# One-column norm sums and a scaled identity that spreads the root, in a kernel of four stacked layers

## The reference

```python
def rmsnorm(x, g):
    y = x * lax.rsqrt(jnp.mean(x * x, axis=-1, keepdims=True) + EPS)
    return y * g

# layers 0 and 1: sh, sc, gate vectors come from silu(c) @ ada_w + ada_b
h = modulate(rmsnorm(x, norm1_g), sh1, sc1)          # h * (1 + sc) + sh
x = x + g1 * (gated Fourier branch + gated retention branch)(h) @ w_out
h = modulate(rmsnorm(x, norm2_g), sh2, sc2)
x = x + g2 * conv_ffn(h)                             # after layer 1: x = rmsnorm(x, final_g)

# layers 2 and 3: the same form of norms, for x and (mostly) for the context
p, u, vs, q, k, v, gates = split(modulate(rms_norm(x, norm1_g), sh1, sc1) @ w_in)
x = x + g1 * (pool mix + spatial gating + neighbourhood attention, gated)(...) @ w_o
x = x + g2 * square(relu(modulate(rms_norm(x, norm2_g), sh2, sc2) @ w1)) @ w2
return rms_norm(x, final_g)
```

## Time and profile before

| what | value |
|---|---|
| median of 3 runs | 2119.51 us (2118.06 to 2119.61) |
| span of the profiled execution | 2116.1 us |
| what lies around the span | the page gives the span alone, no total time of this execution |
| PE busy | 2080.5 us, 98% |
| DVE busy | 1496.3 us, 71% |
| ACT busy | 987.6 us, 47% |
| POOL busy | 392.7 us, 19% |
| mean granted TensorE clock | 0.992 |
| HBM read | 393.09 MB, 186 GB/s over the span |

### The profile page before, as it was taken

How to read it: one execution, slowest core, us unless ns; L and a number is a source line. 1 busy time by engine, 2 the same in 40 slices (tenths; PEclk the granted TensorE clock), 3 DMA queues, 4 the chain that set the end, 5 groups by cost and what they waited for, 6 DMA issues and landing times.

```text
span 2116.1 us, 36942 instructions
## 1 busy us (share of the span) xinstructions
PE 2080.5 (98%) x14236; PEld 1916.5 (91%) x14236; DVE 1496.3 (71%) x2161; ACT 987.6 (47%) x1501; POOL 392.7 (19%) x288
## 2 busy tenths in 40 slices
PE   8999999999999999999999999999999989999998
PEld 7999999999999999999877888888888988999998
DVE  5876888877777899978988524897533466866554
ACT  4444456544445566553245523432232245755453
POOL 0330203210511213224101102130010031121020
PEclk8999999999999999999999999999999999999999
DMA  7876767686675666664544322456632244564552
GB/s 285 293 253 199 253 221 250 239 288 214 213 239 197 212 199 216 197 233 132 184 165 146 108 85 87 137 182 229 197 101 91 81 158 160 203 214 160 183 186 100
DMA packets 109594, 396.36 MB, mean 187 GB/s; under 512 B 12408, under 2 KB 13056, under 8 KB 109056
## 3 DMA queue, kind: packets, MB, share of 16 engines
q1 hardware_dynamic: 108160, 389.99, 54.7%
q0 software_dynamic: 1280, 4.20, 0.6%
HBM read 393.09 MB, written 1.05 MB: 186 GB/s over the span
## 4 chain that ended last, share of the span: by engine, by line
PE 84%; DVE 11%; DMA 2%; ACT 2%; issue 1%; POOL 0%; DVEq 0%; SPq 0%; POOLq 0%; ACTq 0%
PE bank L486 21%; PE bank L488 21%; PE bank L487 21%; DVE w_lo L1435 5%; PE bank L587 2%; PE bank L585 2%; PE bank L586 2%; DMA stage<-in_stream 1%; PE bank L661 1%; PE bank L658 1%; DVE stage L1456 1%; PE bank L606 1%; DVE rstd L1453 1%; PE bank L509 1%; PE bank L877 1%
## 5 line engine op out<-in xcount | busy, mean ns | idle before, releaser
L1435 DVE TENSOR_TENSOR w_lo<-stage,w_hi 128x1024 fp32r<-128x1024 f32 x536 | 705.0, 1330 | 457.2 <-ACT w_hi L1004 456.9
L1004 ACT ACTIVATE w_hi<-stage 128x1024 fp32r<-128x1024 f32 x536 | 565.7, 1059 | 849.0 <-PE bank L488 599.9
L486 PE MATMUL bank<-h_hi,w_hi 128*128 128x256 f32 (+1 forms) x2560 | 788.5, 308 | 6.8 <-DVE w_lo L1435 4.1
L487 PE MATMUL bank<-h_lo,w_hi 128*128 128x256 f32 (+1 forms) x2560 | 782.9, 306 | 0.0
L488 PE MATMUL bank<-h_hi,w_lo 128*128 128x256 f32 (+1 forms) x2560 | 782.9, 306 | 0.0
L486 PEld LDWEIGHTS bank<-h_hi,w_hi 128*128 128x128 f32 x2560 | 489.8, 191 | 36.5 <-DVE w_lo L1435 7.4
L487 PEld LDWEIGHTS bank<-h_lo,w_hi 128*128 128x128 f32 x2560 | 489.8, 191 | 21.6 <-issue 0.5
L488 PEld LDWEIGHTS bank<-h_hi,w_lo 128*128 128x128 f32 x2560 | 489.7, 191 | 21.5
L1456 DVE SCALAR_TENSOR_TENSOR stage<-stage,cvec 128x1024 f32<-128x1024 f32 x188 | 253.8, 1351 | 4.2 <-DMA stage<-in_stream 1.7
L486 PE MATMUL bank<-f_hi,w_hi 128*128 128x256 f32 (+1 forms) x448 | 147.3, 329 | 0.0
L488 PE MATMUL bank<-f_hi,w_lo 128*128 128x256 f32 (+1 forms) x448 | 146.7, 327 | 0.0
(11 more groups left out here) (254 smaller groups left out, 3272.2 us busy)
## 6 DMA issues: line engine op xcount, KB each, us to landing
stage<-in_stream SPq DMA_DIRECT2D x728, 512.0 KB, 4.3
bias<-in_bias POOLq DMA_DIRECT2D x16, 256.0 KB, 3.2
X<-in_x SPq DMA_DIRECT2D x2, 1024.0 KB, 7.0
cvec<-in_cvec SPq DMA_DIRECT2D x3, 512.0 KB, 4.1
decay<-in_decay SPq DMA_DIRECT2D x1, 1024.0 KB, 5.4
out<-X SPq DMA_DIRECT2D x4, 256.0 KB, 2.1
rope<-in_rope SPq DMA_DIRECT2D x2, 256.0 KB, 4.9
wsgu<-in_wsgu SPq DMA_DIRECT2D x2, 256.0 KB
```

The source lines that it names most:

```text
L486: mm(out, w_hi[:, slot, w], xh[:, c, 0:T], start=first, stop=False)
L487: mm(out, w_hi[:, slot, w], xl[:, c, 0:T], start=False, stop=False)
L1004: A(w_hi[:, m % NR, :], stage[:, n % NS, :], ACT.Copy).then_inc(hi_ready, 1)
L1435: do(V.tensor_tensor(w_lo[:, m % NR, :], stage[:, n % NS, :], w_hi[:, m % NR, :].bitcast(F32), ALU.subtract), unit_done, done_value(n))
```

## The change

A norm's sum is taken as one column for each half of its 256 tokens, and not as a row spread over all partitions.

- norm_sums: for each source chunk two products take the place of one, with 128 tokens of the squares as the stationary side and one column of mean_D as the moving one. The result is 128 tokens (on partitions) by 2 columns. The number of source chunks, GpSimd's adds and the waits on them stay.
- root works on 2 columns, and so does the reciprocal. VectorE then writes diag: the identity times the reciprocal column, for each half of the tokens (two tensor_scalar products of 128x128).
- spread_root, new on TensorE: ones (128x128) as the stationary side by diag (256 columns) puts the root of every token in all partitions of a second bank. So each norm has two groups where it had one.
- scaled and final_norm read the root from that bank (root_of); after the eighth chunk VectorE copies one element (root_used) to release it. For the first norm keep_root copies it to rstd, and the chunks read rstd.
- The identity is loaded in SyncE's prologue, behind X and ahead of the weight stream, no longer with the tables of layer 2 (`loaded2` counts 48 where it was 64).
- Where there is padding, 16 products become 4, the spread, and 5.
- The hooks: in dn1 the sums stay before unit 4 and the spread stands before unit 5; in pu of layer 2 nf's sums move one output chunk ahead, from (0, 0, 2) to (0, 0, 1), with the spread at (0, 0, 3); in pu of layer 3 the sums of c1 move from before unit 3 to before unit 2, with the spread before unit 3. The other hooks stay and have the spread two output chunks behind.

In the diff below, the places where only `loaded2` changes are left out.

```diff
-        s = [("n1", 0, 1)]
+        s = [("n1", 0, 2)]
...
-        s += [("wo0", 4, 4), ("wo1", 4, 4), ("n2", 0, 1)]
+        s += [("wo0", 4, 4), ("wo1", 4, 4), ("n2", 0, 2)]
...
-            s += [("nf", 0, 1)]
+            s += [("nf", 0, 2)]
         return s
-    s = [("c1", 0, 1), ("n1", 0, 1)] if layer == 2 else [("n1", 0, 1), ("c1", 0, 1)]
+    s = [("c1", 0, 2), ("n1", 0, 2)] if layer == 2 else [("n1", 0, 2), ("c1", 0, 2)]
...
+        std = sb("std", [P, 2, 2])
+        rcol = sb("rcol", [P, 2, 2])
+        junk = sb("junk", [1, 16])
...
-        std = sb("std", [P, T2], F32, tmp + 16 * KB)
+        diag = sb("diag", [P, 2, 2, P], F32, tmp + 16 * KB)
...
             sp.dma_start(X[:, 0, :, :], t["x"][:, 0, :, :]).then_inc(s["x_loaded"], 16)
+            sp.dma_start(ident[:, :], t["ident"]).then_inc(s["ident_in"], 16)
             for n in range(PRO):
...
-            for dst, name in ((rope2, "rope2"), (rinv, "rinv"), (rotm, "rotm"), (ident, "ident")):
+            for dst, name in ((rope2, "rope2"), (rinv, "rinv"), (rotm, "rotm")):
                 sp.dma_start(dst.ap(), t[name]).then_inc(s["loaded2"], 16)
...
                 added = ADDS[layer, name] + 1 if ADDS[layer, name] else 0
                 open_group(g)
+
+                def add(src, first, last):
+                    for tk in range(2):
+                        at = tok.start + tk * P
+                        ins = mm(bank_of(g)[:, tk:tk + 1], src[:, at:at + P], mean_D[:, 0:1], start=first and tk == 0,
+                                 stop=last, skip_group_check=True)
+                    return ins
                 if added:
                     pe.wait_ge(s["sq_added"], ADDS_BEFORE[layer, name] + ADDS[layer, name])
-                    ins = mm(bank_of(g)[:, 0:S], mean_D[:, :], ssum[:, tok], start=True, stop=added == DC)
+                    ins = add(ssum, True, added == DC)
                     if added == DC:
                         close_group(ins, g)
                 for c in range(added, DC):
                     pe.wait_ge(s["sq_ready"], SQ_BEFORE[layer, name] + c + 1)
-                    ins = mm(bank_of(g)[:, 0:S], mean_D[:, :], sq[:, c % 4, tok], start=not added and c == 0, stop=c == DC - 1)
+                    ins = add(sq[:, c % 4, :], not added and c == 0, c == DC - 1)
                     if c == DC - 1:
                         close_group(ins, g)
                     elif not added:
                         ins.then_inc(s["sq_used"], 1)
+
+            def spread_root(layer, name):
+
+                g = grp(layer, name, 1)
+                out = open_group(g)
+                pe.wait_ge(s["diag_ready"], NORMS.index((layer, name)) + 1)
+                at = diag[:, half_of(name), :, :]
+                close_group(mm(out[:, 0:S].rearrange("p (k t) -> p k t", k=2), ones[:, :], at, start=True, stop=True), g)
 
             def fill_gap(layer, name, n):
...
             norm_sums(0, "n1")
             for n in range(PRO - 1):
                 first_modulation(n).then_inc(s["pro_used"], 1)
+                if n == 0:
+                    spread_root(0, "n1")
...
                     norm_sums(L, "n1")
-                    fill_gap(L, "in", 16)
+                    fill_gap(L, "in", 4)
+                    spread_root(L, "n1")
+                    fill_gap(L, "in", 5)
                 input_products(L, hh, hl)
...
                 norm_sums(L, "n2")
-                fill_gap(L, "up0", 16)
+                fill_gap(L, "up0", 4)
+                spread_root(L, "n2")
+                fill_gap(L, "up0", 5)
                 feature_block(L, "up0", hh, hl, S, h_ready(L, "n2"), after_norm=(L, "n2"))
...
                 feature_block(L, "dn1", u_hi, u_lo, S, nothing,
-                              before={4: lambda: norm_sums(2, "c1")} if L == 1 else None)
+                              before={4: lambda: norm_sums(2, "c1"), 5: lambda: spread_root(2, "c1")} if L == 1 else None)
...
                     half_passes(L, "pu", h_hi, h_lo, [(ctx_part, (2, "c1")), (x_part, (2, "n1"))],
-                                hooks={(0, 0, 2): lambda: norm_sums(1, "nf"), (0, 3, 0): lambda: norm_sums(2, "n1")}, fresh=(1,))
+                                hooks={(0, 0, 1): lambda: norm_sums(1, "nf"), (0, 0, 3): lambda: spread_root(1, "nf"),
+                                       (0, 3, 0): lambda: norm_sums(2, "n1"), (0, 3, 2): lambda: spread_root(2, "n1")}, fresh=(1,))
                 else:
                     feature_block(L, "pu", h_hi, h_lo, T, h_ready(L, "n1"), after_norm=(L, "n1"),
-                                  before={3: lambda: norm_sums(3, "c1")})
+                                  before={2: lambda: norm_sums(3, "c1"), 3: lambda: spread_root(3, "c1")})
...
-                    split_units(L, "wo1", h_hi, h_lo, 0, hooks={(1, 1, 0): lambda: norm_sums(2, "n2")})
+                    split_units(L, "wo1", h_hi, h_lo, 0, hooks={(1, 1, 0): lambda: norm_sums(2, "n2"), (1, 1, 2): lambda: spread_root(2, "n2")})
...
                     norm_sums(L, "n2")
-                    fill_gap(L, "f0", 16)
+                    fill_gap(L, "f0", 4)
+                    spread_root(L, "n2")
+                    fill_gap(L, "f0", 5)
...
                             half_passes(L, "f0", h_hi, h_lo, [(x_part, (2, "n2")), (ctx_part, (2, "c2"))],
-                                        hooks={(0, 2, 0): lambda: norm_sums(2, "c2")})
+                                        hooks={(0, 2, 0): lambda: norm_sums(2, "c2"), (0, 2, 2): lambda: spread_root(2, "c2")})
...
                     base = 32 * (L - 2) + 16 * half
                     feature_block(L, f"d{half}0", f_hi, f_lo, T, count("ff_ready", base))
                     if L == 2 and half:
-                        split_units(L, "d11", f_hi, f_lo, 4, hooks={(1, 5, 0): lambda: norm_sums(3, "n1")})
+                        split_units(L, "d11", f_hi, f_lo, 4, hooks={(1, 5, 0): lambda: norm_sums(3, "n1"), (1, 5, 2): lambda: spread_root(3, "n1")})
                     else:
                         feature_block(L, f"d{half}1", f_hi, f_lo, T, nothing)
                 if L == 3:
                     norm_sums(3, "nf")
+                    spread_root(3, "nf")
...
-                A(std[:, tokens_of(name)], bank_of(g)[:, 0:S], ACT.Sqrt, bias=eps[:, :]).then_inc(taken[g % 8], 1)
+                A(std[:, half_of(name), :], bank_of(g)[:, 0:2], ACT.Sqrt, bias=eps[:, :]).then_inc(taken[g % 8], 1)
...
             def invert(layer, name):
 
-                tok = tokens_of(name)
+                v = half_of(name)
                 wait_taken(dve, grp(layer, name))
                 settle()
-                do(V.reciprocal(rstd[:, tok], std[:, tok]))
+                do(V.reciprocal(rcol[:, v, :], std[:, v, :]))
+                if (layer, name) == NORMS[0]:
+                    dve.wait_ge(s["ident_in"], 16)
+                settle()
+                do(V.tensor_scalar(diag[:, v, 0, :], ident[:, :], rcol[:, v, 0:1], None, ALU.mult))
+                do(V.tensor_scalar(diag[:, v, 1, :], ident[:, :], rcol[:, v, 1:2], None, ALU.mult),
+                   s["diag_ready"], NORMS.index((layer, name)) + 1)
+
+            def root_of(layer, name):
+
+                return rstd[:, 0:S] if (layer, name) == NORMS[0] else bank_of(grp(layer, name, 1))[:, 0:S]
+
+            def keep_root():
+
+                g = grp(0, "n1", 1)
+                wait_filled(dve, g)
+                take(V.tensor_copy(rstd[:, 0:S], bank_of(g)[:, 0:S]), g)
+
+            def root_used(layer, name):
+
+                n = NORMS.index((layer, name))
+                take(V.tensor_copy(junk[0:1, n:n + 1], root_of(layer, name)[0:1, 0:1]), grp(layer, name, 1))
 
             def scaled(layer, name, c):
 
                 base, v, tok = HREADY[layer, name], half_of(name), tokens_of(name)
                 if c >= 4:
                     dve.wait_ge(s["h_ready"], base + c - 3)
-                do(V.scalar_tensor_tensor(tt[:, c % 4, tok], X[:, v, c, :], MUL[:, layer % 2, v, int(name[1]) - 1, c:c + 1],
-                                          rstd[:, tok], ALU.mult, ALU.mult), s["t_ready"], base + c + 1)
+                if c == 0 and (layer, name) != NORMS[0]:
+                    wait_filled(dve, grp(layer, name, 1))
+                ins = V.scalar_tensor_tensor(tt[:, c % 4, tok], X[:, v, c, :], MUL[:, layer % 2, v, int(name[1]) - 1, c:c + 1],
+                                             root_of(layer, name), ALU.mult, ALU.mult)
+                do(ins, s["t_ready"], base + c + 1)
+                if c == DC - 1 and (layer, name) != NORMS[0]:
+                    root_used(layer, name)
 
             def rest(layer, name, c):
...
                 invert(layer, "nf")
                 settle()
                 last_norm = layer == 3
+                wait_filled(dve, grp(layer, "nf", 1))
                 for c in range(DC):
-                    do(V.scalar_tensor_tensor(X[:, 0, c, :], X[:, 0, c, :], col("final2" if last_norm else "final1", c),
```

(7 more changed lines are left out.)

14 lines of the change are left out of this document (7 added, 7 removed).

## The result

Median of four runs 2133.53 us (2127.71 to 2136.39), against 2119.0 of the kernel before: ratio 1.0071 (95% interval 1.0059 to 1.0083), so 0.7% slower. The profiled execution has a span of 2131.4, 15.3 more than before.

A forecast was written before the change was run, and what follows sets the result against it. The prediction took TensorE, 84% of the last-ending chain, to bound the kernel. Terms 3.9 - 2.8 - 0.7 + 1.0 + 3.9 + 0.5 + 2.8 = +8.6 on 2119.51 gave 2128.1 us; own range 2124 to 2132, 8-in-10 range 2117 to 2136.

The forecast's parts named there:

- The sums cost the same: Norm sums on TensorE: four one-column records, 0.42 us, replace two wide ones, 0.43; put at 0.
- The rival that a load hides behind its neighbour: One-column products: hidden loads would bring the 240 records closer, down to 2108.7 us at 0.025 spacing; faster, chance 0.08.
- The chain: Each norm's root to first scaled chunk: 2.29 us becomes 1.60, a gain of 0.7 (0.4 to 0.9).
- the term of -2.8: Four padded norms (n2 of layers 0, 1, 3; n1 of layer 1): each 0.7 us shorter, -2.8 together.
- The end: Last norm, nf of layer 3, which ends the kernel: the same shorter chain, -0.7 us.
- Prologue: Kernel start: spread and root copy 0.8 us, earlier fall of the clock 3.1; +3.9 together.
- The clock's term: Prologue: narrow products start 3.5 us sooner, so half clock comes sooner; 3.1 us, bounds 0 and 3.5.
- c1 of layer 2: Norm beside dn1: the spread before unit 5 delays the first scaled chunk and the weight split behind it; +1.0 us.
- pu of layer 2: Fourth group waits for the bank of nf's root until eight chunks end, TensorE idling 3.6 us; +3.9, the largest term.
- f0 of layer 2: Bank wait delays the first unit by 2 us, swallowed by a later 2.39 wait; the spread stays, +0.5.
- pu of layer 3: Bank wait swallowed by existing idling, but c1's earlier sums leave one unit behind it; +2.8 us, no extra clock cost.
- The rival: More falls of the clock at padded norms or in layer 2's pu, two of five places: 2134 us, chance 0.26.

The follow-up runs named there:

- the second run: The changed kernel with std, rcol and junk placed behind the last tile, so every other tile lies where the kernel before has it: 2143.45 us.
- the third run: The changed kernel with 128 columns of mean_D instead of one in each product of a norm's sum: 2120.36 us.
- the fifth: The changed kernel with 128-column sums, layer 1's nf root copied to release its bank early, and c1's sums before unit 3 of layer 3's pu: 2112.85 us.
- the first run: The kernel before with only 128 unused bytes per partition added behind rstd, moving the tiles behind as the change does: 2110.9 us.
- the eleventh: The kernel before with the same 128 unused bytes behind rstd, measured once more: 2111.42 us.
- the fourth run: The changed kernel with layer 1's nf root copied to release its bank early, and c1's sums back before unit 3 of layer 3's pu: 2122.08 us.

## Why the prediction was right or wrong

The time lay in the range and slower was forecast, and that it lay there is luck: the norms cost 22 us where 8.6 were forecast, and tiles that moved gave 7 back. Without the 7 the time is above 2136, the end of the range, as in the second run (2143.45). Even with them it is above 2132, the end of the likeliest case's own range. Which places would cost, and by which waits, was forecast rightly; what the clock does behind narrow products was not. By its steps:

**The sums cost the same.** Right: a padded norm's ten products take 2.29 us where its five took 2.32. The rival that a load hides behind its neighbour fell: the row of 16 records above (957.76 in the timeline of pu) has 1.93 us from the first start to the last end, 112 ns from one to the next. The prologue's records of the earlier trace rows are also 112 ns apart, and 213 at half clock; the forecast's 0.106 and 0.207 divide a window by a count that takes in the records cut by its edges. The start-to-start floor of 25 ns of the Trainium skill (TensorE: Matmul & The Clock Gate, "Wait — 56ns, not 53.3ns?") is far below what these rows have.

**The chain.** Direction right, size wrong: 0.7 forecast, 0.39 measured at full clock (root to first scaled chunk 1.90 for the 2.29 of the earlier trace rows). The timeline of layer 1's padded norm n1:

```profile
495.72 0.26 ACT L1079 ACTIVATE std<-bank,eps 128x2 f32<-128x2 f32 x1 [0.24 <-PE bank L607]
496.01 0.17 DVE L1537 RECIPROCAL rcol<-std 128x2 f32<-128x2 f32 x1 [0.80 <-ACT std L1079]
...
496.85 0.67 PE L629 MATMUL bank<-diag,ones 128*128 128x256 f32 x2 [0.16 <-DVE diag L1542]
...
497.62 1.26 DVE L1567 SCALAR_TENSOR_TENSOR tt<-X,MUL,bank 128x256 f32<-128x256 f32 x3 [0.93 <-PE bank L629]
```

The root takes 0.26 and not 0.20, diag starts the spread 0.14 after it ends, and from the spread to the first chunk it is 0.77, not 0.64. Two of the four padded norms gained 0.43 and 0.51; the other two, with the clock down, lost 0.65 and 0.45, so the term of -2.8 came out at +0.2. Where the clock stays up, in the third run, the four gain 0.32 to 0.41 each, half of the 0.7. The end gave 0.47 for 0.7. The chunks that read PSUM take 475 ns where those from SBUF took 480, so that they cost nothing more was right. The dearer PSUM source of the Trainium skill (VectorE: DVE Perf Modes, "The TRN2 errata") does not show in these rows.

**Prologue.** +3.9 forecast, +6.4 measured. The step that failed is the clock's: it falls near 10 and not near 12 (0.75 in the window from 8 to 12 is two of its four us at the lower level; before, still had 1.00 to 15.3). The clock's term was 3.1 with a bound of 3.5; from the third run to the changed kernel the stretch grows by 6.1. An estimate from the rows: 5.4 us of narrow work, some 48 records at 112 ns, now ran at 213, which is 4.9 more. What the spread and the copy (0.8 forecast) cost besides cannot be read from the table. The stretch is +0.25 in the third run and +1.85 in the fifth, with the same prologue, and +0.38 and +0.14 in the first and the eleventh, which have the old one. In the changed kernel the timeline reads:

```profile
27.73 0.16 DVE L1617 TENSOR_TENSOR MOD<-bank,cols 128x2 f32<-128x2 f32 x1 [13.53 <-PE bank L657]
...
28.07 0.42 DVE L1553 COPY rstd<-bank 128x256 f32<-128x256 f32 x1
...
32.21 0.79 PE L679 MATMUL bank<-w_hi,h_hi 128*128 128x512 f32 x1 [4.58 <-DVE w_lo L1464]
```

The copy takes the 0.4 that was forecast; the modulations end at 27.7 and not at 25.

**c1 of layer 2.** Right: from the start of its sums to the first scaled chunk it is 3.97 us where it was 2.92, and the wait for the split is 1.07 where it was 0.37; with the spread's 0.43 that is +1.1 for 1.0.

**pu of layer 2.** The mechanism right to the row: an idle 3.44 (forecast 3.6), ended by the one-element copy, behind eight chunks in 3.22 us (forecast 3.2), and the fourth run takes it away. The whole stretch is +7.6 where c1 and pu together had 4.9; the fall of the clock behind the idling, which stood among the rivals, is 1.4 of it (from the third run to the fifth the stretch loses 4.3, 2.85 of that the wait), and the fall at n1's own narrow sums another 1.2.

**f0 of layer 2.** +0.48 without a fall, 0.5 forecast: right. The bank wait is there (1.31 us at 1342.92) and swallowed. With the two falls it is +3.1. Only the first of them stands behind narrow sums.

**pu of layer 3.** +3.5 for 2.8, and by the reason given: the bank wait only splits the idling (2.14 and 4.05 us for 5.96), and unit 2 comes behind it. That the clock would cost the same again was wrong: unit 2 ran at half clock and took 5.1 us for the 2.88 put down. Undone, the stretch is 2.2 shorter than before, since unit 3 then runs at the full clock.

**The rival.** More falls was what happened, for half its reason only: idling in pu and two padded norms, as said, but also n1 and n2 of layer 2, where narrow sums stand between wide products. The argument against it, that only 2.1 of 4.6 us are narrow, does not hold: two of the four padded norms fell with just these 2.1 us. Its 2134 is near the measured 2133.5 by luck. It had two falls at 2.5 to 3.1 us each; the trace has eight more than before besides the longer one in the prologue, the ones that the stretches single out cost 0.6 to 1.7 each, and the tiles took 7 off. The prediction also took a wait of 2.39 us as one that passes without a fall; the first run falls behind the same wait. It gave this case 0.26 where it should have led.

**Left out altogether:** where the tiles lie, -7 us. The diff's three small tiles were read as free. This is the term that the sum put at nothing without a reason.

## What to carry to other kernels

Do not make a product narrower to save time where the trace shows narrow records as far apart as wide ones (112 ns here): with 128 columns the sums took as long and the clock stayed up, which was worth about 10 us. Before a step gets another PSUM group, list who stands on its bank eight groups later, and release a bank that is read many times by copying it once. And when a change adds or moves tiles, run the moved layout alone too, or its effect is booked on the change.

## What the runs showed of the hardware

- TensorE's clock went to its lower level behind one-column products although the engine was busy without a gap: with the padding at one column in three norms of four, with the same padding at 128 columns in none. It is not certain at any one place: the changed norms brought it down behind two, three and four of the four padded norms in the changed kernel, the fourth and the second run.
- The same wait of 2.4 us at the same place, ahead of c2's sums, passed with the clock at 1.00 in the kernel before and ended at 0.50 in the first run.
- VectorE's products of 128x256 with all operands in SBUF took 0.96 us beside GpSimd's adds and 0.48 otherwise; with one operand in PSUM they took 0.48 beside such adds too. Eight of them: 4.72 us before, 4.71 in the fourth run, 3.22 with the root in PSUM.
- The spacing of products of the same size at the full clock depends on where the moving tile lies: 114 or 118 ns for u with 256 columns, 233 or 229 for f with 512, for 128 bytes of shift, the same in every kernel with that layout. The better place for 256 columns is the worse one for 512. In three other layouts the spacing changes from stretch to stretch, and the rule is open.
